# A gated delta net whose two directions become two threads of ten phases, interleaved on every engine

## The reference, cut to what matters

```python
gcum = jnp.cumsum(g, axis=-1)
decay = _masked_exp(gcum[..., :, None] - gcum[..., None, :], incl)
kb = k * beta[..., None]
a = jnp.where(strict, jnp.einsum('nbhik,nbhjk->nbhij', kb, k) * decay, 0.0)
rhs = jnp.concatenate([v * beta[..., None], kb * jnp.exp(gcum)[..., None]], axis=-1)
sol = lax.linalg.triangular_solve(a, rhs, left_side=True, lower=True, unit_diagonal=True)
u, w = sol[..., :dv], sol[..., dv:]

def step(s, inp):
    qc, kc, uc, wc, gc, dc = inp
    v_new = uc - jnp.einsum('bhck,bhkv->bhcv', wc, s)
    g_last = gc[..., -1]
    s_new = s * jnp.exp(g_last)[..., None, None] + jnp.einsum(
        'bhck,bhcv->bhkv', kc * jnp.exp(g_last[..., None] - gc)[..., None], v_new)
    o = jnp.einsum('bhck,bhkv->bhcv', qc * jnp.exp(gc)[..., None], s) + jnp.einsum(
        'bhij,bhjv->bhiv', jnp.einsum('bhik,bhjk->bhij', qc, kc) * dc, v_new)
    return s_new, o
```

## Time and profile before

| | us |
|---|---|
| median of three runs | 3102.23 |
| profiled execution, its own time | 3101.86 |
| its span, first to last instruction | 3100.1 |
| time outside the span | 1.76 |
| from the end of GLA's last output group (281.65) to the first matmul of the merge (796.79) | 515.1 |
| PE busy in the span | 2702.7 (87%) |
| DVE, ACT, POOL busy | 650.1, 561.3, 65.9 |

### The profile page before, as it was taken

One profiled execution on the slowest core, in us unless ns is written; L12 is line 12 of the kernel. 1 busy time (PEld: TensorE's weight loads), 2 busy tenths in 40 slices (PEclk: granted clock), 3 DMA queues, 4 the chain that ended last, 5 costly groups with the idle time before them and its releaser, 6 DMA issues.

```text
span 3100.1 us, 32772 instructions
## 1 busy us (share of the span) xinstructions
PE 2702.7 (87%) x13308; PEld 1974.5 (64%) x13308; DVE 650.1 (21%) x1429; ACT 561.3 (18%) x978; POOL 65.9 (2%) x60
## 2 busy tenths in 40 slices
PE   6999445656888999997999978999999998799998
PEld 2785344555675655654776747867777775486776
DVE  1543333342013111111000081100000004611000
ACT  4623310110112111112001152110010013411000
POOL 0000111101000000000000000000000000000000
PEclk8999789789899999998999988999999998899999
DMA  6144000000256999998443301344434441034430
GB/s 251 68 166 184 4 1 1 1 1 1 116 205 244 423 422 422 422 422 354 149 149 137 138 11 81 138 153 157 149 136 149 151 143 72 1 142 157 149 135 14
DMA packets 71171, 481.87 MB, mean 155 GB/s; under 512 B 7840, under 2 KB 11424, under 8 KB 13600
## 3 DMA queue, kind: packets, MB, share of 16 engines
q1 hardware_dynamic: 65808, 472.46, 38.8%
q10 hardware_dynamic: 5264, 8.00, 0.7%
HBM read 476.23 MB, written 4.19 MB: 155 GB/s over the span
## 4 chain that ended last, share of the span: by engine, by line
PE 82%; DVE 10%; ACT 4%; DMA 2%; issue 2%; POOL 0%; SPq 0%; DVEq 0%; ACTq 0%; POOLq 0%
PE bank L468 80%; ACT arena L1805 3%; PE bank L480 2%; DMA ring<-in_stream 2%; DVE arena L1410 1%; DVE arena L1122 1%; DVE arena L1407 1%; DVE softmax_small L1712 1%; DVE arena L1710 1%; DVE arena L1733 1%; DVE arena L1371 0%; ACT hT L1805 0%; DVE arena L1413 0%; DVE arena L1416 0%; DVE arena L1359 0%
## 5 line engine op out<-in xcount | busy, mean ns | idle before, releaser
L468 PE MATMUL bank<-hT,ring 128*128 128x256 f32 (+1 forms) x2880 | 692.8, 400 | 8.1 <-issue 6.7
L468 PEld LDWEIGHTS bank<-hT,ring 128*128 128x128 f32 x2880 | 548.7, 191 | 143.7 <-issue 74.8
L468 PE MATMUL bank<-arena 128*128 128x128 f32 (+4 forms) x2544 | 446.7, 339 | 203.9 <-ACT arena L1805 69.0
L1805 ACT ACTIVATE arena<-bank 128x512 f32<-128x512 f32 (+1 forms) x420 | 240.2, 572 | 1892.5 <-PE bank L468 1856.5
L468 PEld LDWEIGHTS bank<-arena 128*128 128x128 f32 (+2 forms) x2544 | 343.2, 206 | 293.0 <-issue 153.3
L468 PE MATMUL bank<-hT,ring_late 128*128 128x256 f32 x2240 | 496.7, 381 | 6.7 <-issue 6.7
L468 PEld LDWEIGHTS bank<-hT,ring_late 128*128 128x128 f32 x2240 | 429.3, 192 | 74.6 <-issue 16.4
L468 PE MATMUL bank<-ring,arena 128*64 128x256 f32 (+3 forms) x2432 | 405.8, 428 | 29.5 <-DMA ring<-in_stream 27.3
L468 PEld LDWEIGHTS bank<-ring,arena 128*64 128x64 f32 (+2 forms) x2432 | 223.6, 146 | 195.8 <-issue 132.4
L1122 DVE TENSOR_TENSOR arena<-arena,bank 128x512 f32<-128x512 f32 x60 | 41.3, 688 | 1133.5 <-PE bank L468 1074.2
L468 PE MATMUL bank<-ring_late,arena 128*64 128x256 f32 (+1 forms) x896 | 227.3, 472 | 3.2 <-DVE arena L1455 2.3
(11 more groups left out here) (170 smaller groups left out, 1210.0 us busy)
## 6 DMA issues: line engine op xcount, KB each, us to landing
ring<-in_stream SPq DMA_DIRECT2D x248, 1024.0 KB, 8.7
ring_late<-in_stream SPq DMA_DIRECT2D x198, 1024.0 KB, 8.7
bias_scratch<-arena ACTq DMA_DIRECT2D x12, 256.0 KB, 2.0
arena<-bias_scratch ACTq DMA_DIRECT2D x2, 1536.0 KB, 10.0
constants<-in_con SPq DMA_DIRECT2D x1, 1184.0 KB, 9.3
x_tok<-in_x SPq DMA_DIRECT2D x1, 1024.0 KB, 5.2
arena<-in_ctx SPq DMA_DIRECT2D x1, 1024.0 KB, 6.9
out<-x_tok SPq DMA_DIRECT2D x2, 512.0 KB, 2.7
```

The costliest lines, as they stand in the source:

```text
L468: ins = engine.matmul(out_, lhsT, rhs, start=start, stop=stop, skip_group_check=True)
L1805: engine.activation(o, i, f, **kw).then_inc(*s_.inc(ev))
```

## The change: what it does

Each direction becomes a thread. A chunk of one thread has ten phases: 0 segments and Gram matrix, 1 transposes and the first level, 2 to 7 the other six levels, 8 w, u and w times the state, 9 the state's increment and the outputs. There are 44 slots. Direction 0 starts at slot 0 and direction 1 four slots behind, so in a steady slot direction 0 is at phase p and direction 1 at phase p-4 (mod 10) of its own chunk. In each slot every engine first does the part `delta_first` of direction 0, then that of direction 1, then the parts `delta_second` of both, then the slot's share of other work (`fill_slot`). PE's `four` writes a group of four matmuls into the thread's own bank (2 and 4 for direction 0, 3 and 5 for direction 1), and each thread has its own counts on the semaphores.

Other edits: the cumulated gates of all chunks are formed once, inside GLA (`cumulated`, into `ecum`), not in each step. The four scalings by rows move to POOL as one instruction of 512 columns each (`spread`, arrays `LG`, `KB`, `VB`, `KD` in `ring_late`). DVE's waits for itself mostly go. The last two pieces of `v` (slots 1 and 2) and the two of z (slots 4 and 6), the transposes of `k` (slot 0), of the modulation rows (slot 3) and of `v` (slot 5), the last two convolutions of `v` on DVE (slots 1 and 2), GLA's output norm (slot 3) and q's (slot 4) are done between slots. The column sums of `k` come first, so that k is ready first. The load of block 54, the first into `ring_late` again, waits for the second output (`y_ready` 2) and not for k (`dn_turn`). `q1` is no longer a matmul: the decay matrix is transposed by PE and copied.

```diff
+DN_PHASES, DN_LAG = 10, 4
+DN_SLOTS = [[(d, *divmod(t - DN_LAG * d, DN_PHASES)) for d in range(2) if 0 <= t - DN_LAG * d < 4 * DN_PHASES]
+            for t in range(4 * DN_PHASES + DN_LAG)]
...
-                        sp.wait_ge(sem("dn_turn"), 1)
+                        sp.wait_ge(sem("y_ready"), 2)
...
+            def cumulated():
+
+                engine.wait_ge(*pe.at("dn_gates", 1))
+                for d in range(2):
+                    t = pj_tile()
+                    for i, lhsT in enumerate((U[d], L[d], ones[:, 0:128])):
+                        mm(t[:, 16 * i:16 * i + 16], lhsT, gt[:, :, 4 * d:4 * d + 4], start=True, stop=True,
+                           ev="pj_full" if i == 2 else None)
...
+            def fill_slot(t):
+
+                if t == 0:
+                    turn_tokens(k_)
+                elif t == 3:
+                    for g in range(0, 4, 2):
+                        b = pj_tile()
+                        for i in range(2):
+                            turn_modulation(b[:, 256 * i:256 * i + 256], mrow[:, g + i, :], "pj_full" if i else None)
+                elif t == 5:
+                    engine.wait_ge(*pe.at("dn_v", 1))
+                    turn_tokens(v_)
+                elif t <= 6:
+                    fill()
...
+            def delta_first(step):
+
+                d, s, phase = step
+                ch = DN_CHUNK[s][d]
+                kc = slice(128 * ch, 128 * ch + 128)
+                if phase == 0:
+                    engine.wait_ge(*pe.at("dn_step_gates", 2 + DN_GATE[d, s - 1, 6] if s else d + 1))
+                    if s:
+                        engine.wait_ge(*pe.at("dn_s", DN_S[d, s - 1, 9]))
+                    mm(AB[d][:, :], U[d], flat(LG[d]), start=True, stop=True, ev="dn_segments")
+                    four(CD[d], d, lambda m, h: (k_[:, h, kc],) * 2, "dn_gram")
+                elif phase == 1:
+                    engine.wait_ge(*pe.at("dn_a", DN_0[d, s, 0]))
+                    for h in range(H):
+                        transpose(AB[d][:, 128 * h:128 * h + 128], B[4][:, 4 * d + h, :], ev="dn_at" if h == H - 1 else None)
+                    if s >= 2:
+                        for h in range(H):
+                            transpose(CD[d][:, 128 * h:128 * h + 128], B[1][:, 4 * d + h, :], ev="dn_q1" if h == H - 1 else None)
+                elif phase < 8:
+                    engine.wait_ge(*pe.at("dn_am", DN_LEVELS[step]))
+                    if phase > 2:
+                        engine.wait_ge(*pe.at("dn_xs", DN_XS[d, s, phase - 1]))
+                    else:
+                        engine.wait_ge(*pe.at("dn_x0", DN_1[d, s, 1]))
+                        if s >= 2:
+                            engine.wait_ge(*pe.at("dn_q3_copied", DN_1Q[d, s, 1]))
+                    four(AB[d], d, lambda m, h: (B[4][:, m, :], B[0][:, m, :]), "dn_p")
+                elif phase == 8:
+                    engine.wait_ge(*pe.at("dn_ys", DN_LEVELS[d, s, 7]))
+                    engine.wait_ge(*pe.at("dn_kb", DN_KB[d, s, 3]))
+                    four(AB[d], d, lambda m, h: (KB[d][:, h, :], B[3][:, m, :]), "dn_w")
+                    engine.wait_ge(*pe.at("dn_vb", DN_VB[d, s, 7]))
+                    four(CD[d], d, lambda m, h: (B[3][:, m, :], VB[d][:, h, :]), "dn_u")
+                else:
+                    engine.wait_ge(*(pe.at("dn_vnew", DN_WS[d, s, 8]) if s else pe.at("dn_u_copied", DN_8[d, s, 8])))
+                    if s < 3:
+                        engine.wait_ge(*pe.at("dn_kd", DN_KD[d, s, 5]))
+                        four(CD[d], d, lambda m, h: (KD[d][:, h, :], B[5][:, m, :]), "dn_ds")
...
+                elif 2 <= phase < 8:
+                    engine.wait_ge(*pe.at("dn_p_copied", DN_LEVELS[step]))
+                    if phase > 2:
+                        engine.wait_ge(*pe.at("dn_ys", DN_LEVELS[d, s, phase - 1]))
+                    else:
+                        engine.wait_ge(*pe.at("dn_y0", DN_1[d, s, 1]))
+                        if s >= 2:
+                            engine.wait_ge(*pe.at("dn_q2_copied", DN_1Q[d, s, 1]))
+                    if phase < 7:
+                        four(AB[d], d, lambda m, h: (B[3][:, m, :], B[5][:, m, :]), "dn_x")
+                    four(CD[d], d, lambda m, h: (B[5][:, m, :], B[3][:, m, :]), "dn_y")
+                elif phase == 8 and s:
+                    engine.wait_ge(*pe.at("dn_w_copied", DN_8[step]))
...
+            for t, slot in enumerate(DN_SLOTS):
+                for step in slot:
+                    delta_first(step)
+                for step in slot:
+                    delta_second(step)
+                fill_slot(t)
             clear(bank[6], stop=True)
             clear(bank[7], stop=True, ev="o_full")
-            project(2, LAT)
-            o_sums(1)
+            engine.wait_ge(*pe.at("o_squared", 2))
...
-                for m in range(8):
-                    ts(B[0][:, m, :], L[m // 4], g_of(m), None, ALU.mult).then_inc(*v.inc("dn_step_gates" if m == 7 else None))
-                    engine.wait_ge(*v.last("dn_step_gates" if m == 7 else None))
...
+                elif phase == 1:
+                    engine.wait_ge(*v.at("dn_a", DN_0[d, s, 0]))
+                    mul(of(B[0], d), of(B[4], d), wide(level(0, 1 - d))).then_inc(*v.inc())
+                    tt(of(B[0], d), wide(ident), of(B[0], d), ALU.subtract).then_inc(*v.inc("dn_x0"))
+                    engine.wait_ge(*v.at("dn_at_copied", DN_1[step]))
+                    mul(of(B[3], d), of(B[2], d), wide(level(0, d))).then_inc(*v.inc())
...
-                for m in range(8):
-                    ts(B[4][:, m, :], vtok[:, ch[m // 4], m % 4, :], b_of(m), None, ALU.mult).then_inc(*v.inc())
-                    engine.wait_ge(*v.last())
-                for m in range(8):
-                    ts(B[2][:, m, :], ktok[:, ch[m // 4], m % 4, :], small[:, 40 + m:41 + m], None, ALU.mult).then_inc(*v.inc("dn_scaled" if m == 7 else None))
-                    engine.wait_ge(*v.last("dn_scaled" if m == 7 else None))
...
+                elif 2 <= phase < 8:
+                    if phase < 7:
+                        engine.wait_ge(*v.at("dn_x", DN_XS[step]))
+                        tt(of(B[0], d), of(B[0], d), ps(2 + d), ALU.subtract).then_inc(*v.inc("dn_xs"))
+                    engine.wait_ge(*v.at("dn_y", DN_LEVELS[step]))
+                    tt(of(B[3], d), of(B[3], d), ps(4 + d), ALU.subtract).then_inc(*v.inc("dn_ys"))
...
+            def spread(out_, x, scale):
+
+                return engine.tensor_tensor(out_, x, scale.unsqueeze(2).to_broadcast([P, 4, 128]), ALU.mult)
...
+                if phase == 3:
+                    engine.wait_ge(*g.at("pj_free", TILES["ktok"]))
+                    spread(KB[d], ktok[:, ch], bgc[:, d, 4 * ch:4 * ch + 4]).then_inc(*g.inc("dn_kb"))
+                elif phase == 5 and s < 3:
+                    spread(KD[d], ktok[:, ch], ecum[:, d, 16 + 4 * ch:20 + 4 * ch]).then_inc(*g.inc("dn_kd"))
+                elif phase == 6 and s < 3:
+                    step_gates(d, s + 1)
+                elif phase == 7:
+                    engine.wait_ge(*g.at("pj_free", TILES["vtok"]))
+                    spread(VB[d], vtok[:, ch], beta[:, ch, 4 * d:4 * d + 4]).then_inc(*g.inc("dn_vb"))
...
+                if t == 0:
+                    copy_tiles([ktok[:, c].rearrange("p a b -> p (a b)") for c in range(4)])
+                elif t in (1, 2):
+                    engine.wait_ge(*s_.at("dn_conved", 2 * H + t))
+                    copy_tiles([rawv[:, t - 1, :]])
+                elif t == 3:
+                    copy_tiles([mrow[:, 2 * i:2 * i + 2, :] for i in range(2)])
+                    engine.wait_ge(*s_.at("dn_conved", 3 * H))
+                    act(v_, v_, ACT.Silu, "dn_v")
+                elif t == 5:
+                    copy_tiles([vtok[:, c].rearrange("p a b -> p (a b)") for c in range(4)])
+                elif t in (4, 6):
+                    copy_tiles([hnZ[1][:, t - 4:t - 2, :]], ACT.Silu)
+
...
+                if phase == 0:
+                    engine.wait_ge(*s_.at("dn_segments", DN_0[step]))
+                    act(of(B[1], d), ps(2 + d), ACT.Exp, "dn_d")
+                elif phase == 1:
+                    engine.wait_ge(*s_.at("dn_at", DN_1[step]))
+                    act(of(B[2], d), ps(2 + d), ACT.Copy, "dn_at_copied")
+                    if s >= 2:
+                        engine.wait_ge(*s_.at("dn_q1", DN_1Q[step]))
+                        act(of(B[6], d), ps(4 + d), ACT.Copy, "dn_q1_copied")
+                elif phase < 8:
+                    engine.wait_ge(*s_.at("dn_p", DN_LEVELS[step]))
+                    act(of(B[5], d), ps(2 + d), ACT.Copy, "dn_p_copied")
+                elif phase == 8:
+                    engine.wait_ge(*s_.at("dn_w", DN_8[step]))
+                    act(of(B[0], d), ps(2 + d), ACT.Copy, "dn_w_copied")
+                    engine.wait_ge(*s_.at("dn_u", DN_8[step]))
```

(4 more changed lines are left out.)

433 lines of the change are left out of this document (190 added, 243 removed).

## The result

The changed kernel takes 2870.98 us (median of four runs, 2866.21 to 2872.2) against 3102.32 for the kernel before on the same chip: ratio 0.9252, 95% interval 0.9236 to 0.9268. The forecast was 2875.5, with a range of 2842 to 2920. The profiled execution has a span of 2869.7 instead of 3100.1, 230.4 less.

A forecast was written before the change was run, and what follows sets the result against it. From 281.65 to the merge (515.1 us) a chain passing between engines was the bound. PE's work of 239.9 plus waits, tails and end norm summed to 288.4, a gain of 226.7, so 2875.5 us; range 2842 to 2920.

The forecast's parts named there:

- PE busy: GLA's end to the merge: PE's work at full clock 239.9 us, plus 2 for pipeline tails at bare hops.
- waits before slot 0: Before the delta net's first slot: PE waits 1.3 us for the norm's sums and 1.6 for the sums of q.
- slots 1 to 9: Slots 1 to 6: PE waits for copies of P and, in slot 4, ACT's queue, 4.4 us; slot 9 adds 0.8.
- Size of a group: PE's matmuls in the stage: a group of four takes 0.945 us, the pipeline's tail some 0.06.
- Steady rounds: Ten slots in about 49 us: PE waits 5.0, in bare copies of 0.75 and waits for DVE or POOL.
- POOL and DVE: First level of each chunk and direction: the two engines obstruct each other, half a mask each, 4 us in all.
- exemption: Delta net's subtractions: DVE instructions reading PSUM, with at most one SBUF input, do not contend with POOL; keeps the obstruction near 4.
- Rival (a): Steady rounds: every POOL instruction holds DVE, a round needs 55 us instead of 49; time 2905; chance 0.20.
- Rival (b): Delta net: in-order streams interlock, threads hardly overlap, one chunk is a chain of 36.6 us; time 2968; chance 0.07.
- Rival (c): Delta net: no waits in the slots but some at both ends, 264 us; time 2851; chance 0.16.
- Rival (d): First slots through merge: PE's clock falls to the lower level and stays, work takes twice as long; time 3176; chance 0.04.
- Markers: Profile after: first segments near 299, slot 10 near 376, ten slots 49 to 51 us, merge near 570, clock 0.97 or more.

The follow-up runs named there:

- kernel 2: The changed kernel with a lag of 0 slots instead of 4, so both threads do the same phase in each slot; 2866.11 us, ratio 0.9239.
- kernel 10: The changed kernel with lag 0 and the first gate projection of each of three merges ahead of the branch's; 2831.68 us, ratio 0.9128.
- Kernel 5: The changed kernel with the 30 row scalings of 512 columns on DVE instead of POOL, which keeps the masks; 2881.1 us, ratio 0.9283.

## Why the prediction was right, point by point

The stage was forecast at 288.4 us and took 283.8. I set the forecast's terms against the same quantities of the windows:

| term | forecast | measured |
|---|---|---|
| PE busy (work 239.9, tails 2, sums of the end 2) | 243.9 | 245.05 |
| waits before slot 0 (1.3 and 1.6) | 2.9 | 3.4 |
| slot 0 | 3.4 | 2.3 |
| slots 1 to 9 (4.4 and 0.8) | 5.2 | 5.9 |
| three rounds (15.0, and 4 for POOL and DVE) | 19.0 | 13.9 |
| the second thread alone | 3.5 | 3.85 |
| `cumulated` | 1.0 | 0.7, within GLA |
| idle in the end norm | 9.5 | 9.4 |

A measured wait is a window's length less PE's busy time in it, as 50.30 - 43.95 = 6.35 for the first round, 4.1 and 3.4 for the next two.

- *Size of a group.* 0.945 was wrong: the 3.84 of the earlier trace rows ends with some 0.25 of tail, not 0.06. The starts of successive groups lie 0.90 apart (375.34, 376.24), and 0.92 in the longest rows (the 11 groups from 410.03 to 420.17). On 188 groups that is 5 to 8.5 us less. It doesn't show in the sum because tails were mis-sized the other way: each of PE's 30 waits ends a row with such a tail (a single group is 1.16 or 1.06, not 0.90), and the windows 282.36 to 365.28 have clock 0.90 to 0.97, where the forecast had full clock. The two errors, each of 5 to 9 us, hide each other; that PE's busy time came out within 1.2 is partly luck.
- *Steady rounds.* The bare copies came as walked, 0.75 each; the waits for DVE and POOL that were walked beside them came in fewer places and other sizes. The rounds wait 6.4, 4.1 and 3.4, against 5.0 and a share of the 4 in each; the later ones have output groups that fill.
- *POOL and DVE.* The term of 4 was spread over all chunks. In fact it sits mostly at one place: PE's wait for L1471, 4.7 in all, of which 2.96 in the first round. DVE and POOL around the first:

```profile
403.67 0.68 DVE L1179 TENSOR_TENSOR arena<-arena,constants 128x512 f32<-128x512 f32 x1
404.39 1.78 DVE L1437 TENSOR_TENSOR arena<-constants,arena 128x512 f32<-128x512 f32 x1
406.10 1.52 DVE L1179 TENSOR_TENSOR arena<-arena,constants 128x512 f32<-128x512 f32 x1
407.65 1.63 DVE L1441 TENSOR_TENSOR arena<-constants,arena 128x512 f32<-128x512 f32 x1
409.21 0.67 DVE L1471 TENSOR_TENSOR arena<-arena,bank 128x512 f32<-128x512 f32 x1
```

```profile
404.35 1.27 POOL L1856 TENSOR_TENSOR arena<-arena,constants 128x512 f32<-128x512 f32 x1 [2.52 <-PE bank L490]
405.58 1.50 POOL L1833 TENSOR_TENSOR ring_late<-constants,arena 128x512 f32<-128x512 f32 x1
407.03 1.71 POOL L1856 TENSOR_TENSOR arena<-arena,constants 128x512 f32<-128x512 f32 x1
```

The first level of one thread (L1437, L1441 and the product between) takes 4.9 us where three instructions of 0.69 would take 2.1, and the other thread's subtraction (L1471) is queued behind it. Over the whole stage the subtractions stay at their price:

```profile
L1856 POOL TENSOR_TENSOR arena<-arena,constants 128x512 f32<-128x512 f32 x48 | 65.4, 1363 | 163.0 <-PE bank L490 129.4 <-ACT arena L1880 24.7 <-DVE arena L1437 8.8
...
L1473 DVE TENSOR_TENSOR arena<-arena,bank 128x512 f32<-128x512 f32 x48 | 32.9, 685 | 23.5 <-PE bank L490 23.2
L1471 DVE TENSOR_TENSOR arena<-arena,bank 128x512 f32<-128x512 f32 x40 | 27.4, 684 | 37.0 <-PE bank L490 37.0
...
L1441 DVE TENSOR_TENSOR arena<-constants,arena 128x512 f32<-128x512 f32 x8 | 13.1, 1640 | 0.3
```

(Forms from 300 to 560: busy, mean ns, idle before.) The forecast took the exemption as likely, and the trace shows it: 27 of these 88 subtractions, with one operand in PSUM, overlap an instruction of POOL and take the same 0.69 as the others (at 413.10 beside POOL's of 412.47), where L1441 with two operands in SBUF takes 1.64. With what the Trainium skill says (SBUF — State Buffer, Who interferes with whom), that DVE with two SBUF inputs contends with GpSimd and with one does not, the trace agrees. The trace also has the size, and that POOL pays too: its mask takes 1.27 or 1.71.
- *Rival (a)* fell by that: DVE is busy 28 to 34 us of a round of 50 to 56, where (a) put it at 55. *Rival (b)* was priced at 2968 and the kernel that has no overlap takes 2963, so its chain was sized well and its condition was not met. *Rival (c)* erred in leaving the rounds without waits. *Rival (d)* was excluded by clock 1.00 in the rounds.
- *Markers.* The first segments were forecast near 299 and came at 300.98; slot 10 near 376 came at 379.93; the ten slots from there 49 to 51, measured 50.3; the merge near 570 came at 566.14. The start was 2 to 4 us too early in the forecast, the rounds and the end were too long.

The mechanism held: the threads cover each other's hops and PE's own work is the bound. The weakest step stands beside the forecast: rival (c) counted the lag of four as a help, and the expectation for kernel 2 did so too; it is a small loss.

## What to carry to other kernels

When a chain hops between engines that work in order, and two independent problems go through it hand in hand, give each its own buffers and issue them alternately, one problem's group and then the other's. The chain's waits vanish where the work of one problem on the busiest engine lasts as long as the other's hop. Here a start in step was enough and an offset cost a tail, so price the tail before the benefit. Then look at what the bound engine still waits for at both ends of the stage: work that needs no output of it, as a gate projection before a branch's, was worth almost 10 us in each of three merges, one at the end of this stage, and nothing tried within the rounds was worth more than 5 to 10.

## What the runs showed of the hardware that was not expected

PE's clock behind a wait isn't told by the wait's length alone. Behind 2.39 us of idling a group took 2.08 in kernel 2 and 1.16 in kernel 10. Kernel 5 has both in one execution: 1.16 behind 2.68 and 2.08 behind 2.69. Behind 2.96 the changed kernel went on at 0.92 a group. What decides between the two stays open.

A DVE instruction of 512 columns with both operands in SBUF took 0.68 with POOL idle and 1.52 to 1.78 beside it, more than POOL's whole 1.27. POOL's instructions took 1.50 and 1.71 there; a scaling and a mask without such a neighbour take 1.04 and 1.27. So two engines' worth of such work is not spread by moving half of it to POOL at that moment. The move still paid: kernel 5, without it, is 10 us slower. Most of POOL's instructions fall beside an idle DVE or beside subtractions that read PSUM, which stay at 0.69.
